# A rebuilt opening: tile 1 projected together with the meta tile, and another order of steps in tiles 0 to 2

## The reference

```
hn   = rms_norm(h) * g_mix;   q, k, v, cb, cc, ch = split(hn @ w_in)
a    = sliding-window (128) attention of q, k, v: q and k normalized per head, bias table, sink logits
c    = cb * causal_conv3(cc * ch)
h    = h + concat(rms_norm(a) * g_a, rms_norm(c) * g_c) @ w_out
h    = h + moe(rms_norm(h) * g_ffn)      # 1 of 4 groups, then 2 of 8 experts of that group
out  = h without the meta tokens
```

## Time and profile before

| | |
|---|---|
| median of 3 runs | 2715.59 us (2714.55 to 2716.6) |
| the profiled execution | 2714.85 us |
| its span, first to last instruction | 2713.2 us |
| TensorE busy in the span | 2603.8 us (96%) |
| VectorE, ScalarE, GpSimd busy | 1755.5, 1606.9, 730.5 us |
| mean granted clock of TensorE | 0.986 of full speed |

### The profile page before, as it was taken

How to read it: one execution, slowest core, us unless ns; L and a number is a source line. 1 busy time by engine, 2 the same in 40 slices (tenths; PEclk the granted TensorE clock), 3 DMA queues, 4 the chain that set the end, 5 groups by cost and what they waited for, 6 DMA issues and landing times.

```text
span 2713.2 us, 48839 instructions
## 1 busy us (share of the span) xinstructions
PE 2603.8 (96%) x14284; PEld 1481.0 (55%) x14285; DVE 1755.5 (65%) x3602; ACT 1606.9 (59%) x2598; POOL 730.5 (27%) x905
## 2 busy tenths in 40 slices
PE   4999999999999999999499999999999999999997
PEld 2455555555555555554256666666666666666665
DVE  5677777777777777776554656565655555456652
ACT  7655555655556655554564757675766565467742
POOL 1133232233222232322222222222222222222221
PEclk9899999999999999999699999999999999999999
DMA  8375555665555655555776767766786766657643
GB/s 315 84 170 162 155 159 151 159 168 154 158 153 155 166 161 156 158 150 136 268 227 180 217 191 244 245 207 187 247 247 199 203 188 204 165 178 247 218 124 55
DMA packets 546521, 495.93 MB, mean 183 GB/s; under 512 B 411771, under 2 KB 411932, under 8 KB 545452
## 3 DMA queue, kind: packets, MB, share of 16 engines
q1 hardware_dynamic: 517516, 406.08, 49.7%
q0 software_dynamic: 28960, 89.30, 13.4%
HBM read 309.74 MB, written 88.41 MB: 147 GB/s over the span
## 4 chain that ended last, share of the span: by engine, by line
PE 90%; DVE 3%; DMA 2%; ACT 2%; SPq 1%; issue 1%; POOL 0%; DVEq 0%; POOLq 0%; ACTq 0%
PE psA L1767 15%; PE psB L1767 15%; PE psG L575 11%; PE psF L1767 8%; PE psG L1767 8%; PE psE L575 6%; PE psF L575 6%; PE psD L575 6%; PE psC L575 6%; PE psH L575 3%; PE psC L1775 1%; PE psE L1782 1%; PE psD L1775 1%; PE psA L677 1%; PE psB L677 1%
## 5 line engine op out<-in xcount | busy, mean ns | idle before, releaser
L575 PE MATMUL psG<-wi_all,both_xT 128*128 128x512 f16 x1536 | 344.9, 381 | 11.1 <-DMA both_xT<-x 10.9
L575 PEld LDWEIGHTS psG<-wi_all,both_xT 128*128 128x128 f16 x1536 | 148.7, 98 | 188.1 <-DMA both_xT<-x 11.1
L1767 PE MATMUL psA<-gate_hi,gT_hi 128*128 128x512 f16 x632 | 241.3, 382 | 5.7 <-issue 3.9
L1767 PE MATMUL psA<-gate_lo,gT_hi 128*128 128x512 f16 x632 | 240.5, 381 | 0.0
L1767 PE MATMUL psA<-gate_hi,gT_lo 128*128 128x512 f16 x632 | 240.4, 380 | 0.0
L1767 PE MATMUL psB<-up_hi,gT_hi 128*128 128x512 f16 x632 | 239.5, 379 | 0.0
L1767 PE MATMUL psB<-up_lo,gT_hi 128*128 128x512 f16 x632 | 239.5, 379 | 0.0
L1767 PE MATMUL psB<-up_hi,gT_lo 128*128 128x512 f16 x632 | 239.5, 379 | 0.0
L1846 ACT ACTIVATE up_hi<-wi_all 128x4096 bf16<-128x4096 f32 x62 | 224.4, 3619 | 0.8 <-DMA wi_all<-in_w_up 0.7
L1878 ACT ACTIVATE aT_hi<-psE 128x512 fp32r<-128x512 f32 x79 | 47.2, 597 | 293.5 <-PE psE L1782 293.5
L1984 DVE TENSOR_TENSOR down_lo<-wi_all,down_hi 128x2048 fp32r<-128x2048 f32 x64 | 143.8, 2289 | 102.2 <-ACT down_hi L1859 102.2
(11 more groups left out here) (340 smaller groups left out, 5696.2 us busy)
## 6 DMA issues: line engine op xcount, KB each, us to landing
wi_all<-in_w_gate SPq DMA_DIRECT2D x32, 2048.0 KB
wi_all<-in_w_up SPq DMA_DIRECT2D x32, 2048.0 KB, 8.7
wi_all<-in_w_down SPq DMA_DIRECT2D x32, 2048.0 KB
xt<-in_x SPq DMA_DIRECT2D x32, 512.0 KB, 3.6
um<-u_rows SPq DMA_DIRECT2D x64, 256.0 KB, 2.7
out_rows<-h SPq DMA_DIRECT2D x32, 512.0 KB, 3.0
xres<-in_x SPq DMA_DIRECT2D x31, 512.0 KB, 4.1
hn_rows<-xres SPq DMA_DIRECT2D x31, 512.0 KB, 2.8
```

The lines of the kernel that those rows point to most:

```text
L575: m = nc.tensor.matmul(ps, left[:, l, k, :], weights.half(r, k, n, width), start=(k == opens and j == 0), stop=(k == closes and j == 2))
L1767: m = nc.tensor.matmul(ps[:, :], l[:, k, :], r[:, r_k[n], :], start=(n == 0 and j == 0), stop=(n == len(l_k) - 1 and j == 2))
```

## The change

The opening is written out engine by engine ahead of `schedule`, which now begins at t = 1. Tile 1's x is loaded by ACT's queue while w_in is still loading, normalized before the split of w_in, into another place (`hn_halves`, which is free then), and turned behind the meta tile's. The meta tile is turned into another buffer (`both_mT`) and projected into other banks (psE, psA, psB). TensorE's first projections take, per chunk, K, V, C and H of the meta tile and, two chunks behind, Q, K and V of tile 1. The gains of w_in have their own semaphores, so that the scaling of w_in waits for its own gain only; the output gains are loaded after w_out. The sums of w_out stand in pairs of chunks between ACT's steps for tiles 0 and 1. The router's scales stand between the two `conv_input`s on DVE. The scale of w_out and its whole split are now in t = 1: the scale between `top_scores(1)` and `lower_prob(1)`, chunks 0 to 3 where 4 to 7 were, chunks 4 to 7 after `attended(1)`. POOL does `body(-1)` and `body(0)`, then both remaining all-reduces, and then goes into `schedule`.

```diff
+    x_halves = x16[:, 0], x16[:, 1]
+    def rows_of_x(t):
+        return hn_halves if isinstance(t, int) and t == 1 else x_halves
+    def banks_of(t):
+        return (psE, psA, psB) if isinstance(t, int) and t == 0 else (psH, psC, psD)
...
-        for t in range(-2, 3):
+        for t in range(1, 3):
             body(t)
...
-    rbx, gk = (a, Cs), qsq[:, 0:2 * HD]
+    rbx, gk = (a, Cs), Bs[:, 0:2 * HD]
...                                                   # SP
         def turn_x(t):
-            seen(ph, t - 1)
-            seen(pb, t - 1)
+            if isinstance(t, int) and t == 1:
+                seen(xT_in, 0)
+            else:
+                seen(ph, t - 1)
+                seen(pb, t - 1)
+        load_x(0)
+        load_weights_in()
+        load_gains_in()                  # g_mix, q_norm, k_norm
+        turn_meta()                      # into both_mT
+        load_small()                     # sinks, router biases, g_ffn, conv weights
+        turn_x(1)
+        load_x(2)
+        load_weights_out()
+        load_gains_out()                 # g_out, two loads
+        load_router()                    # waits for band_out, 16 loads
+        turn_k(0)
+        turn_q(1)
+        turn_k(1)
+        store_u(0)
+        turn_x(2)
+        load_x(3)
+        store_u(1)
+        load_shifted(1)
         schedule(sp, body)
...                                                   # TensorE
+            of_meta = ((pkv, psE[:, 0:256], O_K), (pc, psA[:, :], O_C), (ph, psB[:, :], O_H))
+            of_first = ((pq, psG[:, :], 0), (pkv, psH[:, 0:256], O_K))
+            ahead = 2
+            after(pe, xT_in, 0)
+            for k in range(KD + ahead):
+                if k < KD:
+                    chunk(k, both_mT, of_meta)
+                if k == ahead:
+                    after(pe, xT_in, 1)
+                if k >= ahead:
+                    chunk(k - ahead, both_xT, of_first)
...
+        pe.wait_ge(band_sb, HEADS)
+        first_projections()
+        bound_values()
+        project_c(1)
+        project_h(1)
+        project_b(1)
         schedule(pe, body)
...                                                   # ACT, in body(t)
             if isinstance(t, int) and t == 1:
-                split_hi("out", LAST_CHUNKS)
+                split_hi("out", FIRST_CHUNKS)
...                                                   # after drain_c(t + 1, t - 1)
-            if isinstance(t, int) and t == 0:
-                split_hi("out", FIRST_CHUNKS)
+            if isinstance(t, int) and t == 1:
+                split_hi("out", LAST_CHUNKS)
...
+        norm_x(0)
+        bounds("in", FIRST_CHUNKS)
+        after(act, x_hi_s, 0)
+        after(act, x_lo_s, 0)
+        hold(act, held)
+        act.dma_start(xt[:], x2[0:P, :]).then_inc(x_in.sem, 16)
+        bounds("in", LAST_CHUNKS)
+        norm_x(1)
+        split_hi("in", range(KD))
+        norm_x(2)
+        norm_q(1)
+        bounds("out", range(0, 2))
+        norm_kv(0)
+        bounds("out", range(2, 4))
+        upper_k(0)
+        upper_q(1)
+        norm_kv(1)
+        bounds("out", range(4, 6))
+        upper_k(1)
+        drain_c(0, -2)
+        bounds("out", range(6, KD))
+        drain_c(1, -1)
+        drain_b(1)
         schedule(act, body)
...                                                   # POOL
-        pool.wait_ge(bound["out"], 1)
-        pool.partition_all_reduce(rt_stat[:, 2:3], rt_stat[:, 0:1], P, RMAX).then_inc(all_bound["out"], 1)
...
-            if isinstance(t, int) and t == 0:
-                all_partitions("out")
+        body(-1)
+        body(0)
+        pool.wait_ge(bound["out"], 1)
+        pool.partition_all_reduce(rt_stat[:, 2:3], rt_stat[:, 0:1], P, RMAX).then_inc(all_bound["out"], 1)
+        all_partitions("out")
         schedule(pool, body)
...                                                   # DVE, in body(t)
             if attn:
                 top_scores(t)
+            if isinstance(t, int) and t == 1:
+                dve.wait_ge(g_out_in, 32)
+                scale_of("out")
+            if attn:
                 lower_prob(t)
             if isinstance(t, int) and t == 1:
-                split_lo("out", LAST_CHUNKS)
+                split_lo("out", FIRST_CHUNKS)
...                                                   # after attended(t, t - 1)
-            if isinstance(t, int) and t == 0:
-                scale_of("out")
-                split_lo("out", FIRST_CHUNKS)
+            if isinstance(t, int) and t == 1:
+                split_lo("out", LAST_CHUNKS)
...
+        lower_x(0)
+        dve.wait_ge(g_mix_in, 16)
+        scale_of("in")
+        lower_x(1)
+        split_lo("in", range(KD))
+        dve.wait_ge(g_in, 32)
+        scale_of_scores()
+        lower_x(2)
+        sum_q(1)
+        sum_k(0)
+        scale_of_values()
+        lower_v(0)
+        scale_q(1)
+        scale_k(0)
+        lower_k(0)
+        lower_q(1)
+        sum_k(1)
+        lower_v(1)
+        scale_k(1)
+        keep_keys(1)
+        lower_k(1)
+        conv_input(0)
+        scales_of_router()
+        conv_input(1)
         schedule(dve, body)
```

More of the change, by code:

```diff
@@ L502, in body @@
             full = proj and live(t + 1, 1)
-            if proj:
+            if proj and not (first and t == 1):
                 turn_x(t + 1)
[L505 to L511, removed]
+            if not (first and t == 1):
+                load_x(t + 2)
             if first and t == 2:
@@ L577, in split_mm, with first_projections, chunk @@
             return m
[L579 to L583, removed]
+        def first_projections():
+            def chunk(k, rows, groups):
+                for signal, ps, n in groups:
+                    m = split_mm(ps, rows, "in", n, True, (k,))
                     if k == KD - 1:
                         m.then_inc(signal.sem, 1)
+            of_meta = ((pkv, psE[:, 0:256], O_K), (pc, psA[:, :], O_C), (ph, psB[:, :], O_H))
[9 more added lines that the diff above has]
+                    chunk(k - ahead, both_xT, of_first)
         pe.wait_ge(hot_in, 32)
@@ L658, in bound_values @@
                 pe.wait_ge(v_sq, k + 1)
-                m = nc.tensor.matmul(psG[:, 0:P], cst[:, C_ONE:C_ONE + P], w_sq[:, k, :], start=(k == 0), stop=(k == KD - 1))
+                m = nc.tensor.matmul(psF[:, 0:P], cst[:, C_ONE:C_ONE + P], w_sq[:, k, :], start=(k == 0), stop=(k == KD - 1))
             m.then_inc(v_cols, 1)
         def project_c(t):
-            after(pe, c_sb, t - 1)
+            if not (isinstance(t, int) and t == 1):
+                after(pe, c_sb, t - 1)
             after(pe, s_sb, t - 1)
@@ L683, in project_h @@
             after(pe, s_sb, t - 1)
-            after(pe, u_s, t - 1)
+            if not (isinstance(t, int) and t == 1):
+                after(pe, u_s, t - 1)
             split_mm(psD[:, :], both_xT, "in", O_H).then_inc(ph.sem, 1)
@@ L780, in halve, with bounds @@
             s.activation(upper, source, ACT.Copy, scale=rx).then_inc(done.sem, 1)
-        def bounds(n):
+        def bounds(n, chunks=range(KD)):
             unread = splits[n].slots[:, 0, 0:splits[n].n].bitcast(BF16)
-            for k in range(KD):
+            for k in chunks:
                 if n == "in":
@@ L903, in drain_c @@
             after(act, hnT_in, turned)
-            s.activation(Cs[:], psC[:, :], ACT.Copy, scale=inv_in).then_inc(c_sb.sem, 1)
+            if isinstance(t, int) and t == 0:
+                after(act, xT_in, 1)
+            s.activation(Cs[:], banks_of(t)[1][:, :], ACT.Copy, scale=inv_in).then_inc(c_sb.sem, 1)
         def norm_a(t):
@@ L1404, in body @@
             full = proj and live(t + 1, 1)
-            if isinstance(t, int) and t == -1:
-                dve.wait_ge(g_in, 16 * 5)
-                scale_of("in")
-                split_lo("in", range(KD))
-                scale_of_scores()
-            if isinstance(t, int) and t == 0:
-                scales_of_router()
             if isinstance(t, int) and t == 1:
@@ L1437, in body @@
                 sum_k(t + 1)
-                if isinstance(t, int) and t == -1:
-                    scale_of_values()
                 lower_v(t + 1)
```

63 lines of the change are left out of this document (32 added, 31 removed).

## The result

The changed kernel takes 2720.05 us (median of 20 runs, 2716.86 to 2725.16); the kernel before, on the same chip, 2716.41 (2713.90 to 2719.57). The ratio is 1.0016, with a 95% interval of 1.0010 to 1.0022: 0.16% slower, some 4 us. The profiled execution took 2717.95 us (span 2716.0), 3.1 more than that of before; it is the second lowest of the 20. One execution of the first experiment's kernel, at 7742.58 us, is left out of its ratio.

A forecast was written before the change was run, and what follows sets the result against it. Opening bound by tile 1's ACT, DVE and POOL chain to TensorE at 176.03: 2.2 us ahead at the norm, then 5.2 added, 3.0 later; 2714.85 + 3.0 = 2717.9, predicted 2718.0 us, 8-in-10 range 2708.5 to 2724.

The forecast's parts named there:

- POOL's switch: POOL, before tile 1's first `yc` multiply: changing from all-reduce to elementwise code costs 6.9 us, now on the path.
- w_out's split in tile 1: DVE in tile 1: first four chunks from 102.8, 6.05 us; other half before `norm_a(1)`, of which 5.2 us count.
- Split of w_in: Start of w_in's split: 35.3 instead of 33.56, 1.7 us later, with 1.3 for loading tile 1's x and 3.0 for its norm.
- First projections: TensorE's projections of the meta tile and tile 1: Q of tile 1 there at 64.6, against 79.75 before.
- rival three: SP stands again in small loads, tile 1's turns land near 53 instead of 44: 2726 us, chance 0.18.
- ACT from there: ACT from Q of tile 1 to the drain of the meta tile's C: 16.9 us, from 64.6 to 81.5.
- DVE: DVE from 81.5: u(0), router's scales, u(1), bias, then score reductions ending at 97.2, about 12 us ahead of before.
- w_out's scale: DVE, between score reductions and `lower_prob` of tile 1: 2.3 us, to 99.5.
- POOL against DVE: POOL's convolution steps and DVE's `split_lo` alternate in tile 1: done at 116.5 if serial, else 112.8.
- the serial sum: POOL's six steps of 1.26 and four remaining `split_lo` of 0.76 added one after another from 105.2: 116.5.
- Behind it: From tile 1's convolution norm, 2.2 us ahead, w_out's other half adds 5.2: `lower_a(1)` at 137.6, all 3.0 us later.
- Rivals one and two: POOL in tile 1. One: switch counts, alternation does not, 2714.3, chance 0.17. Two: neither counts, 2709.6, chance 0.17.

The follow-up runs named there:

- the first experiment: Changed kernel with w_out's reduction over the partitions moved into the middle of the router's steps: 2716.93 us, ratio 1.0006 to the kernel before.
- the hidden switch: Changed kernel with w_out's reduction early and one 128x1 TENSOR_TENSOR on POOL behind it: 2715.21 us, ratio 1.0003 to the kernel before.
- the first two experiments: Changed kernel with w_out's reduction moved among the router's steps, 2716.93 us; then also with a 128x1 TENSOR_TENSOR on POOL behind it, 2715.21 us.
- the extra matmuls: Changed kernel with B of tile 1 (24 matmuls, 5.2 us) done twice on TensorE ahead of tile 1's scores: 2725.57 us (5 runs), ratio 1.0033.
- the first of the two best kernels: Changed kernel with all edits that helped, POOL's fills issued at about 80 us by plan (74.8 in the run): 2710.91 us, ratio 0.9983.

## Why the prediction was right, step by step

The forecast (2718.0; a loss of about 3 us in the opening, from POOL's switch and w_out's split in tile 1) held: the lost time, its place and its size in the profile. On the way to it two terms were wrong and cancelled, and that was luck: Q came 3.6 us late, and the steps that POOL and DVE share took 1.8 us less than their sum.

- *Split of w_in*: 34.38 for 35.3. The load of x cost 0.5, not 1.3 (the last sum began at 29.23 for 28.74, and at 29.05 to 29.91 in the other kernels); ACT issued it in 0.39 us. So the rule of the Trainium skill that the prediction weighed, "DMA: Bandwidth & Descriptors", section "Issuing engines are not separate DMA queues", agrees with these rows, at a third of the price.
- *First projections*: the step that failed. Q was read at 68.18, not 64.6. The forecast went by a turn of tile 1's x that lands near 44. It landed at 49.6, past the 47 from which rival three said it decides, and TensorE waited for it, rival three's sign. The mechanism was not rival three's second stand of SP in small loads: taking these away gained 1.3 us of landing. It was the 2 MB of POOL's fills, which the prediction had not on its list of transfers: with them elsewhere x was there in time and Q read at 63.4. About half of these 4.7 us is the wait, the other half the granted clock of 0.55 to 0.60 behind it: with the same wait and the clock at 1.00 (the hidden switch) Q was read at 65.92.
- *ACT from there*: 15.2 us for 16.9 (from 68.18 to the end of the drain of C, 83.34). The sums lay partly in ACT's own waits. The drain came 1.8 late in place of 3.6.
- *DVE*: u(0) to the bias 9.6 for 9.8; the reductions ended at 99.05 for 97.2; w_out's scale took 2.04 for 2.3.
- *POOL's switch*: 7.07 for 6.9, behind the all-reduce as said; `yc` at 107.22 for 105.2. On the path it was worth about 2 to 3 of its 7 us, since behind it ACT's half of the split ends next: the first two experiments moved the norm by 3.0 and 5.5 us, of which Q's earlier reading gave 1.0 and 2.3.
- *POOL against DVE*: they alternate, but the six steps took 9.4 us where the serial sum had 11.2 (its terms end at 116.4, not 116.5). This undid the lateness: norm at 116.65 for 116.5. The rule of the Trainium skill, "SBUF — State Buffer", section "SBUF: two separate sides", is borne out in part. The split took 9.66 beside POOL and 6.02 to 6.16 where POOL had finished, but the serial sum, in which one of the two always stands still, was not reached.
- *Behind it*: `lower_a` at 137.60 for 137.6, the last row of the chain at 178.62 for 179.0. From the norm to `lower_a` it is 20.95 us, 15.93 before: w_out's other half is in it with 5.0 us, for 5.2.

Rivals one and two are out by the rows. "This is all the gain there is, and what follows eats it" holds of the score reductions. But the prediction let TensorE's scores of tile 1 lie beside the rest at no cost, and the extra matmuls showed that it has at most some 2 us to spare there.

What stays open: by the ratio the loss is some 4 us, in the profiled execution 3.1. In one profiled run the turn landed at 55 instead of 49.6, so a landing that varies would do it. The four kernels whose turn is in time spread by 3.8 to 6.5 us over 11 runs, the others by 5.3 to 12.4 over 10 to 20 (5.0 over five), which fits but does not show it. How often the turn lands late in the changed kernel was not measured. Nor did a run move the second half of w_out's split alone: its 5 us are read from the rows.

## What to carry to other kernels

A transfer that is moved earlier has to be weighed against every queue's transfers at its new place, POOL's fills too: here 2 MB that nobody waited for cost some 5 us twice, at the first and at the second place. Where an engine's waits vanish and the time does not, follow the chain behind the wait to the next join (here the count of tile 1's routing) before pricing anything. And POOL's switch from all-reduce to elementwise steps can be paid early, with one tiny step behind the last reduction.

## What the runs showed of the hardware

- The switch between an all-reduce and a TENSOR_TENSOR begins at the first instruction of the other kind, behind the waits ahead of it: 92.8 for an all-reduce that ended at 89.2. It took 6.8 to 8.0 us in the runs here. The Trainium skill, "GPSIMD Engine Reference", section 2.1 "Instruction dispatch", gives about 6 us for the first call of a newly loaded kernel, with nothing to see in the profile; the gaps here are one to two us longer.
- Two DMA transposes of 128x1024 took 14.1 and 13.1 us to land beside the fills, 8.9 and 7.5 without these, 6.1 and 5.1 with SP's small loads gone too (the first of the two best kernels).
- TensorE's granted clock fell to 0.50 (1.2 GHz) in the scores of tile 1 whether TensorE had waited before (3.6 us, fills behind the V copies) or not (fills at w_out's landing). In the first projections the stretch with a wait of 3.6 us had it at 0.55, and in two runs with the same wait it stayed higher (0.82 with Q at 67.14, 1.00 with Q at 65.92).
